# A fused two-layer transformer kernel: a new order of work between the attention heads of both layers

## The reference

```python
def first_block(x, c, ...):
    ada = silu(c) @ w_ada + b_ada                      # six vectors of 1024
    h = modulate(rmsnorm(x, g_mix), shift_a, scale_a)
    gq, gk, gv, gr, gg, mq, mk, mv = split(h @ w_in)
    o_gla  = gla_mixer(...)                            # 4 heads, chunked linear attention
    o_gla  = rmsnorm(o_gla, g_gla_out) * silu(gr)      # norm over each head's 128 values
    o_moba = moba_mixer(mq, mk, mv, rel_bias)          # 8 heads, causal softmax with a bias
    x = x + gate_a * (concat([o_gla, o_moba]) @ w_out)
    h = modulate(rmsnorm(x, g_mlp), shift_m, scale_m)
    return rmsnorm(x + gate_m * (square(relu(h @ w_ff1)) @ w_ff2), g_final)

def second_block(x, ...):
    z = rms_norm(x, norm1_g) @ w_in
    attn = dilated_attention(...)                      # 8 heads, softmax
    conv = silu(layer_norm(depthwise_conv(a * sigmoid(b))))
    x = x + concat([attn, conv]) @ w_out
    return x + expert_choice_moe(rms_norm(x, norm2_g))  # 16 experts of 1024 x 2816, 32 tokens each
```

## Time and profile before

| what | value |
| --- | --- |
| median of three runs | 1854.61 us |
| the profiled execution, its own time | 1853.62 us |
| its span, first to last instruction | 1851.9 us |
| TensorE busy | 1353.7 us, 73% |
| VectorE busy | 274.7 us, 15% |
| ScalarE busy | 226.6 us, 12% |
| GpSimd busy | 39.4 us, 2% |
| read from HBM | 647.38 MB |

### The profile page before, as it was taken

One profiled execution on the slowest core, in us unless ns is written; L12 is line 12 of the kernel. 1 busy time (PEld: TensorE's weight loads), 2 busy tenths in 40 slices (PEclk: granted clock), 3 DMA queues, 4 the chain that ended last, 5 costly groups with the idle time before them and its releaser, 6 DMA issues.

```text
span 1851.9 us, 24026 instructions
## 1 busy us (share of the span) xinstructions
PE 1353.7 (73%) x10574; PEld 831.9 (45%) x10574; DVE 274.7 (15%) x559; ACT 226.6 (12%) x530; POOL 39.4 (2%) x64
## 2 busy tenths in 40 slices
PE   6998999999987777476666757566655665756665
PEld 4576888888655334142332414234232322413232
DVE  1215100006952001000010100001000000100001
ACT  1333222012133010000100001010000100000010
POOL 0000000002020000000000000000000000000000
PEclk9999999999998777777777777877777787777778
DMA  9746363341444899999999999999999999999998
GB/s 351 299 163 242 114 250 145 128 182 68 185 187 187 372 436 435 427 430 433 438 428 429 435 429 435 430 435 435 427 431 428 442 422 436 435 431 426 430 441 342
DMA packets 48248, 649.02 MB, mean 350 GB/s; under 512 B 3832, under 2 KB 6336, under 8 KB 31056
## 3 DMA queue, kind: packets, MB, share of 16 engines
q1 hardware_dynamic: 45152, 643.90, 82.4%
q10 hardware_dynamic: 2848, 3.55, 0.6%
q0 software_dynamic: 208, 1.00, 0.1%
HBM read 647.38 MB, written 1.06 MB: 350 GB/s over the span
## 4 chain that ended last, share of the span: by engine, by line
DMA 59%; PE 11%; DVE 1%; ACT 1%; issue 0%; SPq 0%; PEldq 0%; DVEq 0%; ACTq 0%
DMA ring<-in_w 59%; PE ps L1216 11%; DVE arena L1113 0%; ACT arena L678 0%; ACT arena L525 0%; DVE arena L1164 0%; DVE arena L1166 0%; DVE xT L1208 0%; ACT L701 0%; ACT L678 0%; ACT arena L688 0%; ACT arena L687 0%; DVE arena L1183 0%; SPq L369 0%; DVE arena L1079 0%
## 5 line engine op out<-in xcount | busy, mean ns | idle before, releaser
L1216 PE MATMUL ps<-ring,table 128*32 128x352 f32 x4032 | 435.3, 602 | 269.4 <-DMA ring<-in_w 269.3
L1216 PEld LDWEIGHTS ps<-ring,table 128*32 128x32 f32 x4032 | 154.1, 140 | 535.5 <-issue 340.4
L1216 PE MATMUL ps<-ring,arena 128*32 128x256 f32 (+1 forms) x2818 | 197.3, 438 | 148.9 <-DMA ring<-in_w 148.6
L1216 PEld LDWEIGHTS ps<-ring,arena 128*32 128x32 f32 (+1 forms) x2818 | 103.2, 125 | 245.1 <-issue 149.0
L1216 PE MATMUL ps<-hT,ring 128*128 128x256 f32 (+1 forms) x880 | 194.6, 382 | 3.0 <-PE ps L1216 1.4
L1216 PEld LDWEIGHTS ps<-hT,ring 128*128 128x128 f32 (+1 forms) x880 | 165.0, 189 | 30.8 <-issue 5.9
L1216 PE MATMUL ps<-arena,ring 128*128 128x256 f32 (+1 forms) x800 | 175.1, 379 | 1.9 <-ACT arena L627 1.4
L1216 PEld LDWEIGHTS ps<-arena,ring 128*128 128x128 f32 x800 | 151.5, 190 | 23.3 <-issue 2.9
L1216 PE MATMUL ps<-arena 32*128 32x256 f32 (+10 forms) x532 | 96.4, 396 | 31.7 <-DVE xT L1208 12.2
L1216 PEld LDWEIGHTS ps<-arena,hT 128*128 128x128 f32 x512 | 106.3, 320 | 9.4 <-issue 9.4
L1216 PE MATMUL ps<-arena,hT 128*128 (+1 forms) x512 | 108.4, 392 | 1.8 <-DVEq L1192 1.8
(11 more groups left out here) (223 smaller groups left out, 542.8 us busy)
## 6 DMA issues: line engine op xcount, KB each, us to landing
ring<-in_w SPq DMA_DIRECT2D x76, 5632.0 KB, 32.9
ring<-in_w SPq DMA_DIRECT2D x19, 2816.0 KB, 28.4
ring<-in_w SPq DMA_DIRECT2D x35, 1408.0 KB, 31.3
ring<-in_w_ff SPq DMA_DIRECT2D x8, 4096.0 KB, 14.0
ring<-in_w_ada SPq DMA_DIRECT2D x6, 4096.0 KB, 13.8
ring<-in_w_in SPq DMA_DIRECT2D x3, 4096.0 KB, 14.4
ring<-in_w_in SPq DMA_DIRECT2D x5, 2048.0 KB, 19.2
ring<-in_w_out SPq DMA_DIRECT2D x2, 4096.0 KB, 12.8
```

What stands on the lines that cost most here:

```text
L1216: return pe.matmul(o, w, x, start=first, stop=last)
```

## The change

In the first layer:

- ScalarE takes one gate tile in each of the rounds p = 0, 1, 2. In round 2 it takes `gr3` and makes the tanh after that round's exponents; before, `gr2`, `gr3` and the tanh stood at the end of round 1.
- VectorE runs no `gla_root` in round 0, roots 0 and 1 in round 1 and roots 2 and 3 in round 2 (before: 0; 1 and 2; 3). The product of the linear attention's output with these roots goes to GpSimd, a 128x256 instruction for each head, ahead of its gate product. VectorE's `gla_scaled` is gone, and `gla_gated` is now a three-operand instruction that takes the gain in.

In the second layer:

- ScalarE loads the table of exponents right after the layer norm's root, takes `v1` behind the first two heads' exponents, and makes the convolution's tanh in round 1 ahead of the copies of the turned rows (before: in round 0 behind them).
- VectorE inverts the layer norm's root behind the first two `divided` instead of ahead of them.
- TensorE runs no `z_start` for banks 2 and 3. `z_conv(4)` opens them, and VectorE adds the residual when it takes these banks. `z_conv(7)` moves between the two `turned` of the last round, and `z_heads(0)` ahead of the last `weighted`.

```diff
@@ GpSimd
+            for h in range(GH):
+                pool.wait_ge(s["gla_set"], 7 + h)
+                nc.gpsimd.tensor_tensor(oT[:, h, :], oT[:, h, :], rso[:, h * S:(h + 1) * S], ALU.mult)\
+                    .then_inc(s["grs_set"], 1)
             pool.wait_ge(s["sgr_set"], 1)
             nc.gpsimd.tensor_tensor(gr, gr, sgr, ALU.mult).then_inc(s["grs_set"], 1)
@@ ScalarE, first layer
+                if p == 2:
+                    gr_take(3)
+                    link(A(flat(sgr), flat(gr), ACT.Tanh))
+                    A(flat(sgr), flat(sgr), ACT.Identity, bias=1.0).then_inc(s["sgr_set"], 1)
                 for j in (2 * p, 2 * p + 1):
...
-                for h in ((1,), (2, 3), (), ())[p]:
-                    gr_take(h)
-                if p == 1:
-                    link(A(flat(sgr), flat(gr), ACT.Tanh))
-                    A(flat(sgr), flat(sgr), ACT.Identity, bias=1.0).then_inc(s["sgr_set"], 1)
+                if p < 2:
+                    gr_take(p + 1)
@@ ScalarE, second layer
-            take("v1", vn[:, 1, :], bk("v1"), s["v_set"], 2)
+            A(spare, eps, ACT.Exp)
...
+                if p == 0:
+                    take("v1", vn[:, 1, :], bk("v1"), s["v_set"], 2)
+                if p == 1:
                     for m in (0, 2):
                         act.wait_ge(s["cln_set"], m + 2)
                         link(A(flat(csq[:, m:m + 2, :]), flat(mix2[:, 4 + m:6 + m, :]), ACT.Tanh))
...
+                for j in (2 * p, 2 * p + 1):
+                    if p >= 1:
+                        act.wait_ge(s["pw_set"], 2 * p)
+                    take(f"uT{j}", uTb[:, j % 2, :], bk(f"uT{j}"), s["pT_set"], MH + j + 1)
@@ VectorE, first layer
-            def gla_scaled(h):
...
             def gla_gated(h):
-                dve.wait_ge(s["grs_set"], 1)
-                V.tensor_tensor(mix[:, h, :], oT[:, h, :], gr[:, h, :], ALU.mult).then_inc(s["mixg_set"], 1)
+                dve.wait_ge(s["grs_set"], GH + 1)
+                V.scalar_tensor_tensor(mix[:, h, :], oT[:, h, :], vcol("g_gla_out", h), gr[:, h, :], ALU.mult, ALU.mult)
@@ VectorE, second layer
+                divided(2 * p)
+                divided(2 * p + 1)
                 if p == 0:
                     dve.wait_ge(s["cvar_set"], 1)
                     V.reciprocal(lnr, lnr).then_inc(s["crec_set"], 1)
-                divided(2 * p)
-                divided(2 * p + 1)
...
+                if k < 2:
+                    ins = V.tensor_copy(x_k, bk(f"zb{k}"))
+                else:
+                    ins = V.tensor_tensor(x_k, bk(f"zb{k}"), x_k, ALU.add)
@@ TensorE, second layer
+                    opens = c == CT and m in (4, 6)
...
+                if p == 3:
+                    z_conv(7)
                 turned(2 * p + 1)
-                if p == 0:
-                    z_start(2)
-                    z_start(3)
-                for c in ((), (4,), (5, 6), (7,))[p]:
+                for c in ((), (4,), (5, 6), ())[p]:
                     z_conv(c)
+                if p == 3:
+                    z_heads(0)
                 weighted(p)
```

More of the change, by code:

```diff
@@ L852, in _, with gla_root @@
             dve.sem_inc(s["S_set"], 1)
-            def gla_root(q):
-                dve.wait_ge(s["gla_n"], 1 + q // 2)
-                link(V.reciprocal(rso[:, q * S:(q + 1) * S], rso[:, q * S:(q + 1) * S]))
-            def gla_scaled(h):
-                link(V.scalar_tensor_tensor(oT[:, h, :], oT[:, h, :], vcol("g_gla_out", h), rso[:, h * S:(h + 1) * S],
-                                            ALU.mult, ALU.mult))
+            def gla_root(h):
+                dve.wait_ge(s["gla_n"], 1 + h // 2)
+                V.reciprocal(rso[:, h * S:(h + 1) * S], rso[:, h * S:(h + 1) * S]).then_inc(s["gla_set"], 1)
             def gla_gated(h):
-                dve.wait_ge(s["grs_set"], 1)
-                V.tensor_tensor(mix[:, h, :], oT[:, h, :], gr[:, h, :], ALU.mult).then_inc(s["mixg_set"], 1)
+                dve.wait_ge(s["grs_set"], GH + 1)
+                V.scalar_tensor_tensor(mix[:, h, :], oT[:, h, :], vcol("g_gla_out", h), gr[:, h, :], ALU.mult, ALU.mult)                    .then_inc(s["mixg_set"], 1)
             def scored(i):
@@ L902, in _ @@
                     ada_rows(3)
-                    gla_root(0)
                 if p == 1:
@@ L906, in _ @@
                     ada_cols(3)
+                    gla_root(0)
                     gla_root(1)
-                    gla_root(2)
                 if p == 2:
                     headed(1)
+                    gla_root(2)
                     gla_root(3)
-                    gla_scaled(0)
-                    gla_scaled(1)
                 if p == 3:
                     ada_rows(4)
-                    gla_scaled(2)
-                    gla_scaled(3)
                     for h in range(GH):
@@ L1127, in _ @@
                     V.reciprocal(lnr, lnr).then_inc(s["crec_set"], 1)
-                divided(2 * p)
-                divided(2 * p + 1)
-                if p >= 1:
+                else:
                     headed(p - 1)
@@ L1139, in _ @@
                 wait_filled(dve, f"zb{k}")
-                V.tensor_copy(xT_[:, 2 * k * S:(2 * k + 2) * S], bk(f"zb{k}")).then_inc(s["x2_set"], 1)
+                x_k = xT_[:, 2 * k * S:(2 * k + 2) * S]
+                if k < 2:
+                    ins = V.tensor_copy(x_k, bk(f"zb{k}"))
+                else:
+                    ins = V.tensor_tensor(x_k, bk(f"zb{k}"), x_k, ALU.add)
+                ins.then_inc(s["x2_set"], 1)
                 if k >= 1:
@@ L1634, in z_step @@
                     done = last and m % 2 == 1
+                    opens = c == CT and m in (4, 6)
+                    if opens:
+                        wait_emptied(pe, f"zb{m // 2}")
                     ins = mm(bk(f"zb{m // 2}")[:, (m % 2) * S:(m % 2 + 1) * S], wo2[:, c, m * P:(m + 1) * P],
-                             mix2[:, c, :], False, done)
+                             mix2[:, c, :], opens, done)
                     if done and m == C - 1:
@@ L1696, in _ @@
                     scores(p + 1)
+                if p == 3:
+                    z_conv(7)
                 turned(2 * p + 1)
-                if p == 0:
-                    z_start(2)
-                    z_start(3)
-                for c in ((), (4,), (5, 6), (7,))[p]:
+                for c in ((), (4,), (5, 6), ())[p]:
                     z_conv(c)
+                if p == 3:
+                    z_heads(0)
                 weighted(p)
-            for c in range(CT):
+            for c in range(1, CT):
                 z_heads(c)
```

## The result

| | before | after |
|---|---|---|
| median of 5 runs, us | 1855.01 (1854.27 to 1855.59) | 1844.46 (1841.46 to 1848.13) |
| profiled execution, us | 1853.62 | 1841.69 |
| its span, us | 1851.9 | 1839.8 |
| mean granted clock | 0.833 | 0.837 |

What follows compares the result with a forecast made beforehand. Compute bounds it to about 624 us, then a DMA stream that begins when TensorE has used the first expert slots. 4.0 + 4.8 = 8.8 us off 1853.62 gives 1844.8, plus 1.0 for the median 1845.8; range 1840.5 to 1850.2.

Steps and rivals of the forecast that it cites:

- (a): First layer: exponents of heads 4 and 5 start when their maxima are there; TensorE goes on 4.1 us sooner.
- (b): First layer: the clock's low stretch behind TensorE's wait for head 4 goes too, 1.6 us less.
- (c), (d): First layer: less cover later leaves `y` 4.9 us sooner; GpSimd holding a negation makes it 4.0, `y` at 163.95.
- (e): Second layer: without table load and `v1`'s copy ahead, the first exponents start at 522.5, not 524.55.
- (f), (g): Second layer: root's inversion behind the divisions turns head 0 3.4 us sooner; low clock behind that wait goes, 1.6 less.
- (h): Second layer: dropping two identity matmuls saves 1.8 us, but 0.8 comes back, as they covered a copy.
- (i), (j): Second layer: waits of 0.7 us for head 2's diagonal (2.2 with negation held) and 1.5 for head 3 (1.2 held).
- (k), (l): Second layer: head 7's wait for a copy covered, 0.8 us less; second low-clock stretch, 1.6 less if it goes.
- Rival 1: GpSimd holds nothing small and the clock stays up: 12.9 us less, 1841.7; chance 0.27.
- Rival 3: The end doesn't follow, loads hide the gain: 1850.2 if half is lost, 1854.6 if all; chance 0.08.
- Rival 4: Second layer: the convolution's chain on GpSimd delays `z_conv(4)`; slower, 1859 if 15 us late; chance 0.04.
- Rival 2: The clock falls more often, behind new waits in both layers: 5.6 us less, 1849.0; chance 0.16.

Runs made afterwards that it cites:

- e5_exp_only: Kernel before with one move: ScalarE takes the third gate tile, tanh and identity behind the exponents of heads 4 and 5; 1848.41 us, 0.9972.
- e4_again: The changed kernel itself, run once more in a later batch; 1842.27 us, 0.9933.
- e1_first: Kernel before with only the change's first-layer edits, on all engines; 1850.58 us, 0.998.
- e7_noload: Changed kernel without the small added activation behind the root that loads the exponents' table early in the second layer; 1843.78 us, 0.9947.
- e9_gate1: Changed kernel with one edit: gate tile 1 is taken behind the exponents of heads 2 and 3; 1842.15 us, 0.9929.
- e3_narrow: Changed kernel with each 128x2 negation of the maxima made as two of one column; 1841.94 us, 0.9931.
- e6_ident: Changed kernel with banks 2 and 3 opened by the identity matmuls again, behind head 1's turned rows; 1844.5 us, 0.9943.
- e8_more: Changed kernel with one-column negations, gate tile 1 behind the exponents of heads 2 and 3, `z_heads(0)` ahead of head 3's turned rows; 1836.05 us, 0.9909.
- e8_again: The same kernel as `e8_more`, run again in the third batch; 1836.53 us, 0.9905.
- e10_wide: Kernel of `e8_more` with the two-column (128x2) negations back; 1840.63 us, 0.9923.

## Why the prediction was right, step by step

- **(a) Exponents earlier, 4.1.** Right: the wait is 0.30, and the exponents of head 4 start at 148.37. `e5_exp_only` shows that this move alone does it.
- **(b) The low stretch behind it, 1.6.** Gone in the first profile (clock 1.00 at 158). In others it came back later: at 164 in `e4_again`, at 159 in `e1_first`, `e7_noload` and `e9_gate1`. The price is then paid in part again.
- **(c), (d) The hold of the negation, `y` at 163.95.** The hold is shown: head 7's, as the side that I took had it, and the one-column form isn't held (`e3_narrow`). `y` came at 163.40, or 163.52 on the count of before. The 0.4 are the roots, 3.36 for the 3.54 I took the earlier trace rows, and copies ahead of them that were done a little sooner: root 3 ended at 155.95 for 156.35, and the product and the end of the hold with it. As to the rule of the Trainium skill, "SBUF — State Buffer", section "Who interferes with whom": the traces agree that the hold lasts for the whole of GpSimd's instruction (1.35 and 1.74 us, each to the product's end), and here it goes down to two columns. The condition of an even count, on which the prediction leaned, isn't shown: one column isn't held, but no odd count above one was tried.
- **(e) Exponents at the maximum.** Right in time: 517.96, which is 522.53 on the count of before, for 522.5. Wrong in cause for one part: the added activation brings nothing (`e7_noload`), so by elimination the move of `v1` brings all of it.
- **(f), (g) Head 0, 3.4 and 1.6.** Right: turned 4.37 behind the first scores for 7.87 before (528.11 - 520.24), 3.5 less. Diagonals 0.48 for 2.29. The low stretch at 529 is gone.
- **(h) The identity matmuls, 1.8 less 0.8.** The term that failed, though it doesn't enter the sum, which goes by the end-to-end times, where the diagonal sets head 2. The matmuls lay in waits: without them TensorE waits 0.78 and 1.95 instead of 0 and 1.08, and the stretch is the same (`e6_ident`). I had subtracted the first wait and not the lengthening of the second, though (i) in its held form says that the diagonal sets the time there, whatever TensorE does ahead of it.
- **(i), (j) The held case: waits of 2.2 and 1.2.** Measured 1.95 and 1.19. The negation's hold ends with GpSimd's product at 525.17 (529.74 on the count of before, for 529.8), and what follows takes 0.5 less than I reckoned.
- **(k), (l)** Head 7's wait (0.80) is gone, and so is the second low stretch.
- **End to end.** Held, without any low stretch, I had 6.4 less; it is 7.6. Of the 1.2, 0.8 is there by head 4, turned at 536.49 (541.06 on the count of before, for 541.9: the 540.3 of the sum plus the 1.6 for the hold), and 0.3 comes behind it. I then took 1.6 for one low stretch: none came in this profile, nor in the later profiles of the changed kernel or `e3_narrow` between 515 and 575; in `e7_noload` one of 6.8 us came at 528.
- **Sum.** 8.8 forecast, 12.1 in the profiled execution: 1.6 for the low stretch that stayed away, 1.2 in the second layer's order, 0.5 in the first layer. The median's 10.6 is nearer, presumably because other executions have more low stretches, as `e4_again`'s profile has: what I entered as one certain stretch is several uncertain ones. That the first median came within 1.3 us of the forecast is in part luck: the same kernel again had 1842.27, 12.3 less, which is inside the range but outside the forecast's own 1844.0 to 1847.6.
- **Rivals.** Rival 1's time (1841.7) was met by the profiled execution, and its second half (the clock stays up in both stretches) held there, but its first half (no small hold) is false. Rival 3 is out: the end followed within 0.1 us. Rival 4 too: `z_conv(4)` starts at 531.51 without a wait for GpSimd. Rival 2's time (1849.0) is near the slowest run (1848.13); that the clock fell more often in it is not shown, as that execution wasn't profiled.

Open: why the same wait brings the clock down in one execution and not in the next, and so why five or six runs of the changed kernel and its near relatives spread over 3.0 to 8.0 us (the kernel before, over 2.8 to 4.4 in the three batches). No experiment here chooses it. Part of it lies outside the change: the stretch at 24 us, and one near 500 us, between the layers, which lasted 3.4 to 10.2 us; from the start of `y` to the first scores of the second layer the 13 profiles took 350.6 to 356.4. `e8_more` shows that the time shrinks when the waits go; that the spread does isn't shown, for `e8_again` and `e10_wide` both have 3.2.

## What to carry to other kernels

Look first at what stands in an engine's queue ahead of the instruction that the critical engine waits for, though its input is ready: moving three activations behind two heads' exponents gave 4 of the first layer's 4.6 us, dropped matmuls and an early table load nothing, because both lay in time that another wait owned. A GpSimd instruction placed beside VectorE's chain can hold the next `tensor_scalar` between SBUF tiles even if it has only two columns; two single-column ones were not held. And a TensorE wait of 1 to 2 us may cost more than its length where the clock falls behind it: in `e10_wide` 2.2 us of waits cost 4.1. It doesn't always: in `e3_narrow` 1.6 us less of waits didn't show.

## What the runs showed of the hardware

- A `tensor_scalar` of 128x2 in SBUF (0.17 to 0.19 us) took 1.35, 1.74 and 1.14 us beside GpSimd's products; 128x1 took 0.15 at the same places, and a `reciprocal` of 128x2 0.15 at the first of them.
- A table load (1.28 us) doesn't wait for the semaphore of the activation behind it: it ran from 515.65, and the input was ready at 517.4 (`e7_noload`).
- `scalar_tensor_tensor` between SBUF tiles: two took 2.36 beside a GpSimd product, 1.00 without.
- The clock's fall behind a wait of 1 to 2 us is not fixed by the wait: with 1.56 us in both, it fell in one execution and not in another; with 1.20 us at 24 us, in 7 of 13. There the same 48 matmuls took 12.40 with a stretch at 1.2 GHz and 10.72 without.
